# A 32-token group of h: three bf16 pieces stored from the keys phases, or f32 rows stored and cut on chip ahead of each group

## The reference, cut to what matters

```
h  = RMSNorm_pre2(x) * (1 + scale2(c)) + shift2(c)
q  = (h @ wq)                          # 8 heads x 2 halves of 128
s  = q . subkeys                       # top 16 of 128 in each half
expert, gate = top 16 of the 256 sums, softmax
act = gelu(u_tab[expert] . h)          # 8 heads x 16 experts a token
out = sum(gate * act * v_tab[expert])  # 128 experts a token
```

## Time and profile before

| | us |
|---|---|
| median of 3 runs | 4244.95 (4240.91 to 4259.92) |
| the profiled execution | 4242.17 |
| its span on the core | 4240.4 |
| VectorE busy | 2485.9 (59% of the span) |
| TensorE busy (matmuls) | 3207.4 (76%) |
| GpSimd busy | 1622.4 (38%) |
| ScalarE busy | 793.6 (19%) |

### The profile page before, as it was taken

How to read it: one execution, slowest core, us unless ns; L and a number is a source line. 1 busy time by engine, 2 the same in 40 slices (tenths; PEclk the granted TensorE clock), 3 DMA queues, 4 the chain that set the end, 5 groups by cost and what they waited for, 6 DMA issues and landing times. The chain is left out here.

```text
span 4240.4 us, 46656 instructions
## 1 busy us (share of the span) xinstructions
PE 3207.4 (76%) x15717; PEld 1723.2 (41%) x15717; DVE 2485.9 (59%) x7746; ACT 793.6 (19%) x1291; POOL 1622.4 (38%) x1372
## 2 busy tenths in 40 slices
PE   6999987875698877877788777777666676666676
PEld 4898876764265542521255343243111111111111
DVE  2553553238854656777765656677776555555554
ACT  4233322342123222210123112111000000000000
POOL 2101104434365644542355544353333333333332
PEclk9999998977799987977899888798666666666666
DMA  5001106534899999998999999999999999999998
GB/s 219 32 31 62 52 22 217 202 104 155 331 373 395 392 407 367 375 377 346 371 402 411 390 393 405 383 402 366 369 395 388 414 409 405 412 413 404 413 414 338
DMA packets 224168, 1352.42 MB, mean 319 GB/s; under 512 B 28631, under 2 KB 38167, under 8 KB 81726
## 3 DMA queue, kind: packets, MB, share of 16 engines
q0 software_dynamic: 156672, 1140.92, 66.7%
q1 hardware_dynamic: 67262, 208.51, 13.4%
HBM read 1319.52 MB, written 29.81 MB: 318 GB/s over the span
## 5 line engine op out<-in xcount | busy, mean ns | idle before, releaser
L1117 DVE CUSTOM_DVE_ANT_0 peer_uv<-peer_uv,all_PS 128x512 f32<-128x512 f32 x2176 | 1435.4, 685 | 1108.9 <-PE all_PS L1055 561.8
L1038 POOL DMA_INDIRECT peer_uv<-in_uv,peer_idx x1088 | 1039.1, 955 | 1485.4 <-PE all_PS L1075 1170.6
L1055 PE MATMUL all_PS<-peer_hT,peer_sel 96*128 96x512 bf16 x2176 | 979.1, 466 | 816.6 <-DVE peer_halves L1117 765.5
L1055 PEld LDWEIGHTS all_PS<-peer_hT,peer_sel 96*128 96x128 bf16 x2176 | 205.1, 101 | 1641.7 <-DVE peer_halves L1117 1273.1
L1075 PE MATMUL all_PS<-peer_uv,peer_zw 128*32 128x512 f32 x4352 | 843.9, 876 | 2.0 <-DVE peer_zw L1137 2.0
L921 POOL TENSOR_TENSOR flow_w_lo<-flow_w,flow_w_hi 128x1024 fp32r<-128x1024 f32 (+1 forms) x204 | 460.7, 2262 | 544.8 <-ACT flow_w_hi L914 544.4
L1091 ACT ACTIVATE peer_ge<-peer_pre 128x4 f32<-128x4 f32 x272 | 55.8, 205 | 2089.4 <-DVE peer_pre L1123 2089.3
L1075 PEld LDWEIGHTS all_PS<-peer_uv,peer_zw 128*32 128x32 f32 x4352 | 155.5, 143 | 433.4 <-issue 431.1
L941 PE MATMUL all_PS<-mix_h_hi,flow_w_hi 128*128 128x384 f32 (+1 forms) x672 | 283.8, 422 | 37.1 <-POOL flow_w_lo L921 31.9
L914 ACT ACTIVATE flow_w_hi<-flow_w 128x1024 fp32r<-128x1024 f32 (+1 forms) x204 | 203.6, 1004 | 339.5 <-PE all_PS L943 169.4
L942 PE MATMUL all_PS<-early_h_h_low,flow_w_hi 128*128 128x384 f32 (+1 forms) x672 | 226.2, 337 | 0.0
(11 more groups left out here) (307 smaller groups left out, 4627.8 us busy)
## 6 DMA issues: line engine op xcount, KB each, us to landing
flow_w<-in_w_gate_ab SPq DMA_DIRECT2D x48, 512.0 KB
flow_w<-in_w_query SPq DMA_DIRECT2D x48, 512.0 KB
flow_w<-in_w_conv SPq DMA_DIRECT2D x36, 512.0 KB
peer_uv<-in_uv,peer_idx POOLq DMA_INDIRECT x1088, 10.9
peer_uv<-in_w_ada SPq DMA_DIRECT2D x8, 2048.0 KB, 8.6
stream_heads_w<-in_w_heads SPq DMA_DIRECT2D x24, 512.0 KB, 4.9
flow_w<-in_w_proj_b SPq DMA_DIRECT2D x24, 512.0 KB
flow_w<-in_w_out SPq DMA_DIRECT2D x24, 512.0 KB
```

Source lines behind the costliest of these rows:

```text
L1038: self.nc.gpsimd.indirect_dma_start(out=self.uv[:, n % self.NUV, :], out_offset=None, in_=self.A["uv"], in_offset=bass.IndirectOffsetOnAxi ...
L1055: nc.tensor.matmul(PS[:, f, :], self.sel[:, c:c + 1].broadcast_to([3 * GR, P]), self.hT[:, g % self.NH, f * 512:(f + 1) * 512], start=True ...
L1117: nc.vector.tensor_tensor_reduce(part, part, PS[:, f, :], 1.0, 0.0, ALU.mult, ALU.add, self.halves[:, d, f, e:e + 1]).then_inc(M["dotted"], 1)
```

## The change

h is stored once a tile as f32 rows, in the order in which the gather takes the tokens (four DMAs of 128 KB a full tile, in steps 0 to 2 of the keys phase). The cutting into pieces is gone from keys, with its two ScalarE and two GpSimd operations a tile. A group is now 32 tokens that follow each other, so two buffers of `hT` do. For each of the 34 groups SyncE loads 32 rows of f32 (one DMA of 128 KB, 28 tokens ahead), ScalarE rounds them to the first piece (20 ahead), VectorE subtracts (18 ahead), ScalarE rounds to the second (16 ahead), and VectorE copies the second to its partitions and subtracts for the third (13 ahead). The operations cover 32 partitions and 1024 elements. Group 0 is made in steps 1 to 4 of the first pick phase.

```diff
-    NUV, NZ, ND, NH, AHEAD = 10, 3, 4, 5, 4
+    NUV, NZ, ND, NH, AHEAD = 10, 3, 4, 2, 4
...
+        self.due = lambda n, early: [g for g in range(1, T // GR) if max(GR * g - early, 0) == n]
...
-            if c == 0 and f == 0:
-                pe.wait_ge(self.h_in[g % self.NH], 48 * (g // self.NH) + 48)
+            if m == 0 and f == 0:
+                pe.wait_ge(M["pieces"], g + 1)
...
+    def fetch_rows(self, sp, g):
+
+        u = self.tokens[GR * g][0]
+        at = GR * g - self.before[u]
+        assert u in self.ready_tiles
+        if g:
+            sp.wait_ge(self.M["pieces"], g)
+        sp.dma_start(self.rows[:, :], self.A["h2"][u, at:at + GR, :]).then_inc(self.M["rows_in"], 16)
+
+    def first_piece(self, act, g):
+
+        act.wait_ge(self.M["rows_in"], 16 * g + 16)
+        if g >= self.NH:
+            act.wait_ge(self.M["h_spread"], 2 * GR * (g - self.NH + 1))
+        self.nc.scalar.activation(self.hT[0:GR, g % self.NH, :], self.rows[:, :], ACT.Copy).then_inc(self.M["first"], 1)
+
+    def rest_of_first(self, dve, g):
+
+        dve.wait_ge(self.M["first"], g + 1)
+        self.nc.vector.tensor_tensor(self.rows[:, :], self.rows[:, :], self.hT[0:GR, g % self.NH, :], ALU.subtract).then_inc(self.M["rest"], 1)
+
+    def second_piece(self, act, g):
+
+        act.wait_ge(self.M["rest"], g + 1)
+        if g:
+            act.wait_ge(self.M["pieces"], g)
+        self.nc.scalar.activation(self.second[:, :], self.rows[:, :], ACT.Copy).then_inc(self.M["second"], 1)
+
+    def last_pieces(self, dve, g):
+
+        dve.wait_ge(self.M["second"], g + 1)
+        self.nc.vector.tensor_copy(self.hT[GR:2 * GR, g % self.NH, :], self.second[:, :])
+        self.nc.vector.tensor_tensor(self.hT[2 * GR:3 * GR, g % self.NH, :], self.rows[:, :], self.second[:, :],
+                                     ALU.subtract).then_inc(self.M["pieces"], 1)
...
+            for g in self.due(n, 20):
+                self.first_piece(act, g)
+            for g in self.due(n, 16):
+                self.second_piece(act, g)
...
+            for g in self.due(n, 18):
+                self.rest_of_first(dve, g)
+            for g in self.due(n, 13):
+                self.last_pieces(dve, g)
...
-                if g >= self.NH:
-                    sp.wait_ge(M["h_spread"], 2 * self.last_of[self.groups[g - self.NH]] + 2)
-                for piece in range(3):
-                    sp.dma_start(self.hT[piece * GR:(piece + 1) * GR, g % self.NH, :],
-                                 A["pieces"][t, piece, j * GR:(j + 1) * GR, :]).then_inc(self.h_in[g % self.NH], 16)
-                self.loaded += 1
+            for g in self.due(n, 28):
+                self.fetch_rows(sp, g)
...
-                if j - 1 in cut:
-                    i, e = cut[j - 1]
-                    src, made = ((first, one), (third, three), (first, four))[e]
-                    sp.wait_ge(made, i + 1)
-                    sp.dma_start(A["pieces"][part.tiles[i], e, 0:R[i], :], src[0:R[i], :]).then_inc(saved[e], 16)
...
+                if j < nt:
+                    width = R[j] // GR
+                    for q in range(width):
+                        sp.dma_start(A["h2"][part.tiles[j], 0:R[j], :].rearrange("(c q) d -> c q d", q=width)[:, q, :],
+                                     m_rows[q * GR:(q + 1) * GR, j, :]).then_inc(saved, 16)
...
-                    if e == 0:
-                        pool.wait_ge(one, i + 1)
-                        nc.gpsimd.tensor_tensor(here, here, first[0:R[i], :], ALU.subtract).then_inc(two, 1)
-                    if e == 2:
-                        pool.wait_ge(three, i + 1)
-                        pool.wait_ge(saved[0], 16 * (i + 1))
-                        nc.gpsimd.tensor_tensor(first[0:R[i], :], here, third[0:R[i], :], ALU.subtract).then_inc(four, 1)
...
-                    if e == 0:
-                        if i:
-                            act.wait_ge(saved[2], 16 * i)
-                        nc.scalar.activation(first[0:R[i], :], here, ACT.Copy).then_inc(one, 1)
-                    if e == 1:
-                        act.wait_ge(two, i + 1)
-                        if i:
-                            act.wait_ge(saved[1], 16 * i)
-                            act.wait_ge(four, i)
-                        nc.scalar.activation(third[0:R[i], :], here, ACT.Copy).then_inc(three, 1)
```

More of the change, by code:

```diff
@@ L998, in __init__ @@
         self.hT = sc.sb("hT", [3 * GR, self.NH, D], BF16)
+        self.rows, self.second = sc.sb("rows", [GR, D]), sc.sb("second", [GR, D], BF16)
         self.sel, self.sel_in = sc.sb("sel", [3 * GR, GR], BF16), sc.sb("sel_in", [3 * GR, GR])
         self.y = sc.sb("y", [P, D])
-        names = "sel_in ready idx_set h_spread dotted summed gelled weighed v_mm y_out y_saved".split()
+        names = "sel_in ready idx_set rows_in first rest second pieces h_spread dotted summed gelled weighed v_mm y_out y_saved".split()
         self.M = {n: sc.sem(n) for n in names}
         self.uv_in = [sc.sem(f"uv_in{b}") for b in range(self.NUV)]
-        self.h_in = [sc.sem(f"h_in{b}") for b in range(self.NH)]
         self.tokens = []
-        self.groups = []
         for u in range(NT):
             g = rows(ORDER[u]) // GR
-            self.groups += [(u, j) for j in range(g)]
             self.tokens += [(u, c, j) for c in range(GR) for j in range(g)]
         self.before = [next(n for n, k in enumerate(self.tokens) if k[0] == u) for u in range(NT)] + [T]
-        self.last_of = {g: max(n for n, k in enumerate(self.tokens) if (k[0], k[2]) == g) for g in self.groups}
-        self.h_at = [max([self.before[u] - 24, 0] + ([self.last_of[self.groups[g - self.NH]] + 1] if g >= self.NH else []))
-                     for g, (u, j) in enumerate(self.groups)]
-        assert all(self.h_at[g] <= self.before[u] + j for g, (u, j) in enumerate(self.groups))
-        assert self.h_at == sorted(self.h_at)
+        self.due = lambda n, early: [g for g in range(1, T // GR) if max(GR * g - early, 0) == n]
         self.at = {e: 0 for e in ("pool", "pe", "act", "dve", "sp")}
-        self.loaded = 0
         self.stored = ORDER.index(NT - 1)
@@ L1145, in turn @@
             u = self.tokens[n][0]
-            while self.loaded < len(self.groups) and self.h_at[self.loaded] <= n:
-                g = self.loaded
-                t, j = self.groups[g]
-                assert t in self.ready_tiles
-                if g >= self.NH:
-                    sp.wait_ge(M["h_spread"], 2 * self.last_of[self.groups[g - self.NH]] + 2)
-                for piece in range(3):
-                    sp.dma_start(self.hT[piece * GR:(piece + 1) * GR, g % self.NH, :],
-                                 A["pieces"][t, piece, j * GR:(j + 1) * GR, :]).then_inc(self.h_in[g % self.NH], 16)
-                self.loaded += 1
+            for g in self.due(n, 28):
+                self.fetch_rows(sp, g)
             if u == self.stored + 1 and n == self.before[u] + 4:
@@ L1806, in keys_phase @@
         R, nt = part.rows, len(part.tiles)
-        first, third = sc.sb("first", [P, D], BF16), sc.sb("third", [P, D], BF16)
         sub = sc.sb("sub", [P, 2 * PH, NK])
@@ L1810, in keys_phase @@
         s1, s2 = sc.sb("s1", [P, 2, nt, NK]), sc.sb("s2", [P, nt, NK])
-        one, two, three, four = (sc.sem(q) for q in "one two three four".split())
-        saved = [sc.sem(f"saved{q}") for q in range(3)]
+        saved = sc.sem("saved")
         sub_in, q_out, s_mm, s_out, own, listed = (sc.sem(q) for q in "sub_in q_out s_mm s_out own listed".split())
@@ L1819, in keys_phase @@
         turns = Turns(lo, hi, NJ)
-        cut = {3 * i + e: (i, e) for i in range(nt) for e in range(3)}
         @block.sync
@@ L1829, in _ @@
                     w.bring(sp, w0 + j + w.pairs)
-                if j - 1 in cut:
-                    i, e = cut[j - 1]
-                    src, made = ((first, one), (third, three), (first, four))[e]
-                    sp.wait_ge(made, i + 1)
-                    sp.dma_start(A["pieces"][part.tiles[i], e, 0:R[i], :], src[0:R[i], :]).then_inc(saved[e], 16)
-            for e in range(3):
-                sp.wait_ge(saved[e], 16 * nt)
+                if j < nt:
[3 more added lines that the diff above has]
+                                     m_rows[q * GR:(q + 1) * GR, j, :]).then_inc(saved, 16)
+            sp.wait_ge(saved, 16 * (part.n // GR))
         @block.gpsimd
@@ L1988, in _ @@
                 fin.bring(sp, 0, ended)
+            if u0 == 0:
+                gat.fetch_rows(sp, 0)
             for j in range(NJ):
@@ L2024, in _ @@
                 gat.gelu(act, upto(j))
+                if u0 == 0 and j == 1:
+                    gat.first_piece(act, 0)
+                if u0 == 0 and j == 3:
+                    gat.second_piece(act, 0)
                 if j == FIN + 1:
@@ L2110, in _ @@
                 gat.dots(dve, upto(j))
+                if u0 == 0 and j == 2:
+                    gat.rest_of_first(dve, 0)
+                if u0 == 0 and j == 4:
```

(5 more changed lines are left out.)

10 lines of the change are left out of this document (2 added, 8 removed).

## The result

The changed kernel took 4259.96 us (median of 17 runs, 4246.01 to 4270.17) against 4249.32 for the kernel before on the same chip (17 runs): ratio 1.0019, 95% interval [1.001, 1.0027]. A second timing gave 1.0015 [1.0003, 1.0028]. By these ratios the change costs 0.15 to 0.2%, 6 to 8 us (the two medians of the first timing lie 10.6 us apart); the forecast was -2 us. The time lies inside the stated range, but the change is a loss and not a gain.

What follows compares the result with a forecast made beforehand. It took the DMA engines to bound the last phase, with 86 us of DMA idle time in earlier stages. -8 -5 -2 +4 +9 = -2 on 4242.17 gave 4240; the median's 2.8 above made 4243, range 4213 to 4270.

Steps and rivals of the forecast that it cites:

- Part 1: SyncE's loads and stores while the DMA engines are full: 3.14 MB less, -8 us, ends 0 and -14.
- Part 2: SyncE's queue at tile ends: weight loads no longer stand behind waiting loads of h pieces, -5 us, ends 0 and -10.
- Part 3: Keys phase: two ScalarE and two GpSimd operations a tile go, so gathers start earlier; -2 us, ends 0 and -13.
- Part 4: First pick phase: making group 0 delays the first indices, +4 us, ends +2 and +6.
- Part 5: VectorE's new work, 33 groups x 2.9 us: a third felt in keys and pick, +9 us, ends 0 and +29.
- rival B: Keys and pick: VectorE's insertions break the ring of ten gather buffers, +31 us, 4276; chance 0.15.
- Rival B's second mechanism, the port: Where weights are streamed: VectorE operations beginning inside a GpSimd subtraction take 1.8 us more, 13 us in all.
- my upper end: SyncE's saved bytes: -14 us, if rows of 2 KB cost more each MB than the queue's mean.
- Rival A: Stages before the last phase: idle DMA time comes back, -34 us, 4211; chance 0.21.
- Rival C: ScalarE's first rounding waits for late rows ahead of the gelu, +17 us, 4260; chance 0.05.
- The first gather near 1046: Sign expected in the profile after: the first gather, at 1041.7 before, would start near 1046.
- such longer issues from the copies: GpSimd's gather issues: by the port rule VectorE's copies would also delay them; left out of the sum.

Runs made afterwards that it cites:

- no_dve: The changed kernel with VectorE's three operations a group left out, second and third pieces of h zero: 0.9958 of the kernel before.
- the second dose: The changed kernel with each of VectorE's three new operations a group issued twice, same result: 1.014 of the kernel before, 52 us above the changed kernel.
- bytes_back: The changed kernel with the saved bytes loaded and stored again, in rows of 2 KB, used by nobody: 1.0056 of the kernel before.
- ordered_pieces: The kernel before, pieces still made in keys but stored in token order and loaded 24 tokens ahead: 0.9976 of the kernel before, repeated 0.9981.
- hold_back: The changed kernel with SyncE's old waits at the tile ends put back: 1.0025 of the kernel before, 3 us above the changed kernel.

## Why the prediction was wrong, point by point

The sum was -2: a gain of 15 (parts 1 to 3) and a cost of 13 (parts 4 and 5). Measured, the gain is 18 (no_dve) and the cost 23 to 26 (no_dve against the changed kernel), which leaves +6 to +8. The sign was lost in part 5.

- **Part 5, the failed step: "I take a third: +9."** It measured 19 to 22 (23 to 26, less part 4's 4; with the intervals, 12 to 30). Two things in it were wrong. The ten groups of keys and pick cost 11 to 16 us in the profiles, half of their 31 us and not a third; in the pick phase of part 1 two groups cost 7 us, their full work. Six gathers in flight and a quarter of idle time don't absorb that. And the rest, put at nothing because mix, merge, out and norm are 60% busy, is not nothing: the median of no_dve leaves 3 to 11 us for it. There single profiles scatter too much (-1 to +8 us), but the second dose shows it, with 16 to 26 us in those stages beside 18 to 23 in keys and pick. The only cover that held is the last phase, which was argued from a wait for data and not from a share. That is most of rival B: it names 1.0 us a group as the point from which it decides; the 33 groups cost 0.6 to 0.7.
- **Rival B's second mechanism, the port,** is in the trace, and not where rival B put it. On VectorE the three operations take 104.1 us where their medians give 96.9, so 7 us come from cases such as the 3.09 us of L1093, where 1.21 is usual. On GpSimd the gather issues are 17.7 us longer (1055.7 against 1038.0). The rival had 13 us for VectorE alone. How much of the 19 to 22 us goes back to these meetings and how much to VectorE's plain time stays open.
- **Part 4** came as priced, 4.1 us.
- **Part 1, bytes: -8, measured nearer -16,** with 8 at the edge of what the intervals allow. The mechanism was right, the price per MB too low: in the last phase, where it shows most clearly, bytes_back gives 4.6 to 5.9 us a MB, against the queue's own 2.72. (Over all it is 3.6 to 3.9 for the whole 4.47 MB, and 5.1 to 5.4 if only the 3.14 MB of part 1 count.) What such loads do while they run is to be seen in the trace of before at the tile that begins at token 832 (3546 to 3566 us: packets, MB, share of 16 engines):

```profile
q0 software_dynamic: 894, 6.51, 88.3%
q1 hardware_dynamic: 501, 0.87, 13.7%
```

In the same 20 us ordered_pieces, with no such load there, shows:

```profile
q0 software_dynamic: 1153, 8.40, 101.3%
```

0.87 MB of SyncE's (nine loads of pieces, 0.59 MB, and the first of a load of x) displace 1.89 MB of the gather's. At 2.41 us a MB (20.26 / 8.40) that is 4.6 us, 5.2 for each MB, where the queue's own share says 3.1 (13.7% of 20 us for 0.87 MB). The gather's rows themselves became slower beside them, 2.71 us a MB. So in that stretch the queue's share understates what the loads take from others; my upper end was nearer. That this is why bytes_back costs 16 us isn't shown: ordered_pieces moves the same bytes as the kernel before, only at other times, and its last phase is hardly shorter (1002.3 against 1003.7 and 1002.4).

- **Part 2, SyncE's hold: -5, measured -8 to -10 for the whole tile end** (ordered_pieces). Two events carry it, but the one at token 448, a wait of 15.8 us, had not been looked up: I scaled the smaller one. The mechanism was half of it. The hold alone gives 3 back in hold_back, not told from nothing; the rest needs the late loads too.
- **Part 3, what leaves keys: -2**, measured -3 with an interval from -8 to +3 (the first rounding stayed in). The small value fits.
- Singly measured, the gains add to 27 to 30 us, and no_dve gives 18. Each figure carries 5 to 8 us of uncertainty; how they divide the 18 stays open.
- **Rival A** didn't happen: what came back was 18 us, not its 42, and VectorE spent it again. **Rival C** didn't either: no wait for the rows but the one in the first pick phase.
- The first gather near 1046 came at 1054.6 in one profile and at 1046.4 in the other; 8.7 us of the first figure are scatter ahead of the change.

On the ports the Trainium skill (SBUF — State Buffer, "Who interferes with whom") gives the shared pair as an exclusive lock. The trace agrees: L1093 has a maximum of 3.09 us, the copy L1105 one of 2.60, and 28 gather issues end some 0.8 us after a subtraction that they met. The prediction expected such longer issues from the copies; the trace has them at the subtractions, which last longer.

The version that beats both kernels keeps the cutting where it was, on GpSimd and ScalarE in keys, and takes only the tokens' order from the change: 0.9976 and 0.9981 in two timings. It still moves all the bytes that the change saved, and has none of VectorE's new work.

## What to carry to other kernels

A busy share is no cover: work put on an engine whose results others wait for in program order is paid for in part or in full even at 60% busy, unless a wait for data stands behind it in the trace. Ask of every wait on a DMA-issuing queue what is queued behind it, and list all places where it bites before scaling one. And price bytes in a full stretch by putting them back, not by their queue's own share: here that share gave half of what bytes_back measured.

## What was not expected of the hardware

- On VectorE 32 partitions of 1024 f32 take 1.208 us, 128 partitions 1.224; on GpSimd 2.136 and 2.137. Cutting h by groups of 32 instead of tiles of 128 multiplies the time of that work by four; this had been assumed, and is now shown.
- Small loads, most of them in rows of 2 KB, beside a stream of 8 KB rows slow that stream from 2.41 to 2.71 us a MB while both engines' shares add to 1.02.
- A VectorE subtraction of 32 x 1024 elements holds back a gather issue of GpSimd that begins beside it until some 0.8 us after its own end: 1.98 us for an issue instead of 0.94.
- Doubling 104 us of work that cost about 24 made it cost about 76. The price of an insertion rose with what had been inserted already.
